# A hybrid decoder block on one core: another order of the first turnings, an earlier third product, later requests for the sums of h, and two sign products on ScalarE

## The chip, the cores and the metric

The kernel runs on one core of a Trainium2 chip. The metric is device time in microseconds (us), from start to end of one execution, for one problem size: 1024 tokens of 1024 channels, batch 1, all values float32.

## What is computed

The reference is one residual block with two token mixers side by side. Cut to what matters here:

```
mod = silu(c) @ w_ada + b_ada                       # shift, scale, gate
h = rmsnorm(x, norm_pre) * (1 + scale) + shift
u_pool, z_pool, u_ssm, z_ssm, g_pool, g_ssm = split(h @ w_in)        # 1024 x 6144
y_pool = causal_pool_mixer(u_pool, pool_w, pool_scale) * silu(z_pool)
y_ssm = s5_mixer(u_ssm, a_re, a_im, log_dt, b, c, d, glu) * silu(z_ssm)
merged = sigmoid(g_pool) * (y_pool @ w_branch_pool) + sigmoid(g_ssm) * (y_ssm @ w_branch_ssm)
out = x + gate * rmsnorm(merged @ w_out, norm_post)
```

The state-space mixer needs, for each of 64 groups and 64 states, powers and rotations of exp(dt * lambda). These tables ("coefficients") depend on small parameters only, and are made in the kernel.

## The kernel before

All large products are made with three matmuls each: both operands are split in a high part, rounded to the type that the matrix engine takes at full rate, and a low part, the rest; the products high x high, high x low and low x high are added in PSUM. ScalarE makes a high part by a copy (`split_hi`, `h_high`, `t_high`, `pair_high`), VectorE a low part by a subtraction (`split_lo`, `split_h`, `t_low`, `pair_low`). A product of one tile of 128 output channels takes eight steps (`k_step`, L1849), one for each tile of 128 input channels; a step is six matmuls of 512 columns.

The order of each engine's work is written out by hand, one list per engine, and semaphores join the lists. The lists that count here:

**First stage.** x comes in eight tiles of tokens. TensorE turns it to channels first by multiplying with diagonal matrices that hold the row scale (`transposed(k, tiles)`, L1874: tile k of the channels, eight matmuls). Turned tiles 0 and 1 lie in PSUM banks `ps0` and `ps1`, which products 0 and 1 use later; 2 to 7 go by turns through `psb` and `psa`, and ScalarE takes each out with `xt_out(k)` (L1003). Meanwhile VectorE sums the rows of `ada` (shift and scale) for tile k, ScalarE forms `h_of(k)` and `h_high(k)`, VectorE `split_h(k)`, and only then can step k of a product run. TensorE's list is: the turnings 0 to 3 for the first four token tiles, then for the last four, then for each k the step k of product 0 and of product 1 and the turning k + 4; the eight steps of product 2 stand behind steps 5 to 7 of the others (`third`). Product 2 uses `psa`, and its weights are split into `wx_hi`, `wx_lo`, which lie in the memory of `x_tok`, so that `split_hi(2)` waits for all turnings.

**Products 3 to 8** (`FIRST`: seven more of the gate, `gs`, and `zs 0`) follow each other. Weights of product n are split while product n-1 or n-2 runs; `split_hi(n)` stands in ScalarE's list behind the copy out of product n-2 (`evac`).

**Coefficients.** Between the splits, VectorE computes sine, cosine, magnitudes, factors and powers, 64 to 512 columns per operation (`reduced_angles` to `in_out_coefficients`, L530 to L644). When `cos_sin` has set `angle_ready`, GpSimd computes the rotations (`rotations`, L646, 78 operations) into another part of `coef`, and sets `tabled`. SyncE then stores `coef` (L732), after `coef_ready` and `tabled`. `coef` overlies `pair_raw0`, so that `load_pair(0)` waits for the end of that store.

**Sums of h.** The next eleven pairs of products are made by a Strassen-like scheme: seven half products P1 to P7 for each pair of output tiles, in the order P1, P2, P6, P5, P7, P4, P3. P5, P6, P7 and P4 need sums of quarters of h: `t_sums(k)` (VectorE, four operations), `t_high(k)` (ScalarE, 2048 columns) and `t_low(k)` (VectorE), for k = 0 to 3. The weights' side needs `sum1` to `sum4`, `pair_high` and `pair_low` per half product. P1 and P2 use h itself. TensorE's list has a wait for all four `t_low` ahead of the first P1. P2 of the first pair takes bank `ps1` and waits until ScalarE has copied out product 8 (`evac(("zs", 0))`, which stands in its list behind `pair_high` of P1, P2, P6 and P5).

Of the kernel before, what the change touches and what calls it, by code (L numbers as in the profile page):

```python
# [82 lines left out]
X_TILES_ACT, X_TILES_DVE = ((0, 1, 3), (4, 6, 7)), ((2,), (5,))  # L83

# [63 lines left out]
def build(nc, x, c_d, cols_d, consts_d, a_re_d, a_im_d, log_dt_d, bc_d, w_ada_d, wstream_d, pool_d, w_out_d, out):  # L148
    ctx = ExitStack()
    with ctx:  # L150
# [59 lines left out]
        wx_hi = at("wx_hi", [P, KT, P], b_at, F32R)  # L210
        wx_lo = at("wx_lo", [P, KT, P], b_at + TILE, F32R)
# [112 lines left out]
        xt = [ps[0], ps[1]] + [psb, psa] * 3  # L324
# [308 lines left out]
        def in_out_coefficients(steps):  # L633

            do, tt, ts, cmul, _ = s5_steps(nc.vector, steps)
            pr, pi, f_re, f_im = pw_re, pw_im, par["f_re"], par["f_im"]

            bf = lambda a: a.unsqueeze(2).broadcast_to((P, G, 8))
            cmul(coef[:, :, 0:8], coef[:, :, 8:16], pr[:, :, 1:9], pi[:, :, 1:9], bf(f_re), bf(f_im),
                 tmp_a[:, :, :], tmp_b[:, :, :])  # L640
            do(ts(coef[:, :, 8:16], coef[:, :, 8:16], sign, -1.0, ALU.mult, ALU.mult))

            do(ts(coef[:, :, 16:24], pr[:, :, 0:8], sign, None, ALU.mult))
            ts(coef[:, :, 24:32], pi[:, :, 0:8], -1.0, None, ALU.mult).then_inc(coef_ready, 1)  # L644
# [28 lines left out]
        def _(sp):  # L673
# [40 lines left out]
            for k in range(KT):  # L714
                if k in (1, 2):
                    load_w(k - 1)
                for f in range(2):
                    sp.dma_start(ada[:, 2 * (k // 4) + f, :, k % 4, :],
                                 w_ada_d.rearrange("(s k) p m -> k p s m", s=2)[k][:, :, f * HALF:f * HALF + HALF]).then_inc(ada_in[k], 16)
            load_w(2)  # L720
# [9 lines left out]
            sp.wait_ge(coef_ready, 1)  # L730
# [241 lines left out]
        def _(act):  # L972
            fn = nc.scalar.activation

            def split_hi(p):

                act.wait_ge(raw_in[p % 2], 16 * (p // 2) + 16)
                if p == 2:
                    act.wait_ge(xt_done, KT)
                elif previous(p) is not None:  # L980
                    act.wait_ge(mm_done, previous(p) + 1)
                fn((wx_hi if p == 2 else w_hi[p % 2])[:, :, :], raw[p % 2][:, :, :], ACT.Copy).then_inc(hi_done, 1)  # L982
# [20 lines left out]
            def xt_out(k):  # L1003

                act.wait_ge(xt_done, k + 1)
                fn(h_full[k][:, :], xt[k][:, :], ACT.Copy).then_inc(xt_taken, 1)

            def h_of(k):

                if k < 2:  # L1010
                    act.wait_ge(xt_done, k + 1)
                    src = xt[k]
                else:
                    act.wait_ge(xt_taken, k - 1)
                    src = h_full[k]
                act.wait_ge(mod_ready, 2 * k + 2)
                fn(h_full[k][:, :], src[:, :], ACT.Identity, bias=s_col[:, k:k + 1],
                   scale=g_col[:, k:k + 1]).then_inc(h_ready, 1)
# [6 lines left out]
            split_hi(0)  # L1025
            h_of(0)
            h_high(0)
            xt_out(2)
            split_hi(1)
            h_of(1)  # L1030
            xt_out(3)
            h_high(1)
            for k in range(2, KT):
                h_of(k)
                h_high(k)
                if k + 2 < KT:
                    xt_out(k + 2)
                if k == 5:
                    split_hi(2)
            act.wait_ge(h_done, KT)  # L1040
# [15 lines left out]
            for n in range(KT):  # L1056
# [7 lines left out]
                if n == 5:  # L1064
                    t_high(0)
                elif n == 6:
                    for k in range(1, 4):
                        t_high(k)
# [46 lines left out]

            pair_high(0, P1)
            pair_high(0, P2)
            pair_high(0, P6)
# [180 lines left out]
        def _(dve):  # L1299
# [59 lines left out]
            for k in range(KT):  # L1359
                scale_sum(k)  # L1360
                if k == 1:
                    split_h(0)
                shift_sum(k)
                if k > 1:
                    split_h(k - 1)
                if k < 2:
                    split_lo(k)
                if k == 6:
                    split_lo(2)
            split_h(KT - 1)  # L1370
            reduced_angles(steps)
            sine(steps)
            cosine(steps)
            split_lo(3)
# [34 lines left out]
            t_sums(0)  # L1409
            t_low(0)  # L1410
            t_sums(1)
            split_lo(8)
            t_sums(2)
            dve.wait_ge(tabled, 1)
            t_sums(3)
            for k in range(1, 4):
                t_low(k)
# [155 lines left out]

            sum1(0)
            sum2(0)
            pair_low(0, P1)
            pair_low(0, P2)
# [263 lines left out]
        def _(pe):  # L1841
# [32 lines left out]
            def transposed(k, tiles):  # L1874

                if k >= 4:
                    pe.wait_ge(xt_taken, k - 3)
                for t in tiles:
                    if k == 0:
# [6 lines left out]
            def step(n, k):  # L1886

                u = ("gs", n)
                if k == 0:
# [3 lines left out]
                    elif n == 2:  # L1893
                        pe.wait_ge(xt_taken, KT - 2)
# [5 lines left out]
            for tiles in (range(0, 4), range(4, CH)):  # L1900
                for k in range(4):
                    transposed(k, tiles)
            third = {5: (0, 1), 6: (2, 3), 7: (4, 5, 6, 7)}
            for k in range(KT):
# [4 lines left out]
                if k + 4 < KT:  # L1909
                    transposed(k + 4, range(CH))  # L1910
# [50 lines left out]
            pe.wait_ge(t_done, 4)  # L1961
            for j in range(NP):
                half_product(j, P1)
                half_product(j, P2)
                part_a(CHUNK_AT.get((j - 1, "b")))
# [184 lines left out]
```

## Time and profile before

| what | value |
|---|---|
| median of 3 runs | 972.71 us (972.57 to 974.25) |
| the profiled execution | 971.08 us, of which the span of the profile 969.3 us |
| TensorE busy | 941.6 us, 97% of the span |
| VectorE busy | 655.7 us, 68% |
| ScalarE busy | 348.6 us, 36% |
| GpSimd busy | 42.0 us, 4%, all of it between 68 and 113 us |
| granted clock of TensorE | 0.999 of full speed |
| chain that ended last | 89% on TensorE, 8% on VectorE |

The profile lists for each engine when an instruction started and how long it took, and, where the engine sat idle before it, how long and which instruction released it. Instructions of one engine overlap a little at their ends, so that the distance between two starts is often 0.1 us less than a duration. "The chain that ended last" goes back from the last instruction through whatever released each step. TensorE is busy in nearly all of the span, so the first question for any edit is which of its few idle stretches it touches.

### The profile page before, as it was taken

The page shows a single profiled execution, that of the slowest core. Times are in us where ns is not written, and L with a number is a line of the kernel's source. Part 1 is how long each engine was busy: PE and PEld are TensorE (multiplying, and loading weights), DVE is VectorE, ACT ScalarE, POOL GpSimd, SP SyncE. Part 2 cuts the span into 40 slices and gives each one's busy share as a digit, 9 for nine tenths or more (in the row PEclk, how much of TensorE's full clock was granted, in tenths as well). Part 3 has the DMA queues.
Part 4 walks back from the last instruction along what each step waited for, and adds up shares of the span by engine and source line. Part 5 has one row for each costly group of instructions (what it writes and reads, how often), then busy time and mean ns, then how long its engine had stood idle before and what let it go on. Part 6 is the DMA issues. An engine that isn't in the chain of part 4 may idle for free.

```text
span 969.3 us, 11612 instructions
## 1 busy us (share of the span) xinstructions
PE 941.6 (97%) x4448; PEld 789.1 (81%) x4448; DVE 655.7 (68%) x916; ACT 348.6 (36%) x404; POOL 42.0 (4%) x82
## 2 busy tenths in 40 slices
PE   3899989999999999999999999999999999999997
PEld 3788868888888888888888888888888888787886
DVE  5989898998888868766887667664344444355233
ACT  5841252223433344544454544631122231133111
POOL 0019600000000000000000000000000000000000
PEclk9999999999999999999999999999999999999999
DMA  9732463444455459657566544886542255322222
GB/s 346 293 135 84 161 223 140 155 153 153 155 188 190 164 198 260 200 169 216 173 198 200 164 139 135 278 327 226 174 166 109 95 220 192 130 88 87 87 87 87
DMA packets 95687, 168.27 MB, mean 174 GB/s; under 512 B 37648, under 2 KB 54160, under 8 KB 95632
## 3 DMA queue, kind: packets, MB, share of 16 engines
q1 hardware_dynamic: 86272, 163.07, 49.6%
q10 hardware_dynamic: 9360, 4.46, 2.1%
q8 instruction: 35, 0.57, 0.2%
q14 instruction: 20, 0.16, 0.1%
HBM read 118.21 MB, written 49.28 MB: 173 GB/s over the span
## 4 chain that ended last, share of the span: by engine, by line
PE 89%; DVE 8%; DMA 1%; ACT 1%; SPq 1%; issue 0%; DVEq 0%; ACTq 0%
PE ps L1855 49%; PE ps L1958 17%; PE ps L2058 8%; PE psb L1958 5%; PE ps L2004 2%; PE psb L1993 1%; PE psb L1991 1%; PE psa L1979 1%; PE psa L1927 1%; PE psa L1855 1%; DMA x_tok<-in_x 1%; DVE t_lo L1403 1%; DVE w_lo L1309 1%; DVE mod_out L1313 1%; PE psb L1927 0%; PE psa L1881 0%
## 5 line engine op out<-in xcount | busy, mean ns | idle before, releaser
L1855 PE MATMUL ps<-bop,w_hi 128*128 128x512 f32 x1312 | 352.6, 390 | 3.8 <-DVE bop L1357 2.2
L1855 PEld LDWEIGHTS ps<-bop,w_hi 128*128 128x128 f32 x1312 | 245.1, 188 | 55.6 <-issue 2.8
L1855 PE MATMUL ps<-bop,w_lo 128*128 128x512 f32 x656 | 202.0, 389 | 0.0
L1855 PEld LDWEIGHTS ps<-bop,w_lo 128*128 128x128 f32 x656 | 123.2, 188 | 25.6
L1309 DVE TENSOR_TENSOR w_lo<-raw,w_hi 128x1024 fp32r<-128x1024 f32 x49 | 60.1, 1227 | 57.6 <-ACT w_hi L982 57.4
L982 ACT ACTIVATE w_hi<-raw 128x1024 fp32r<-128x1024 f32 x49 | 51.7, 1057 | 94.3 <-PE ps L1855 84.4
L1958 PE MATMUL ps<-bop,r_hi 128*128 128x512 f32 x208 | 64.1, 389 | 0.0
L1958 PE MATMUL ps<-t_hi,r_hi 128*128 128x512 f32 x140 | 55.2, 394 | 0.0
L1958 PE MATMUL ps<-t_hi,r_lo 128*128 128x512 f32 x140 | 54.6, 390 | 0.0
L1958 PE MATMUL ps<-t_lo,r_hi 128*128 128x512 f32 x140 | 54.5, 389 | 0.0
L2058 PE MATMUL ps<-wo_hi,y_hi 128*128 128x512 f32 x128 | 49.9, 390 | 0.4 <-DVE wo_lo L1785 0.4
L2058 PE MATMUL ps<-wo_lo,y_hi 128*128 128x512 f32 x128 | 49.8, 389 | 0.0
L2058 PE MATMUL ps<-wo_hi,y_lo 128*128 128x512 f32 x128 | 49.8, 389 | 0.0
L1089 ACT ACTIVATE r_hi<-r_f 128x512 fp32r<-128x512 f32 x44 | 25.4, 622 | 67.0 <-DVE r_f L1510 65.5
L1958 PEld LDWEIGHTS ps<-bop,r_hi 128*128 128x128 f32 x208 | 39.0, 188 | 8.3 <-issue 0.3
L1773 DVE SCALAR_TENSOR_TENSOR y_raw<-gt,y_raw 128x1024 f32<-128x1024 f32 x8 | 9.8, 1226 | 47.9 <-ACT gt L1048 47.9
L1958 PE MATMUL ps<-bop,r_lo 128*128 128x512 f32 x104 | 40.5, 389 | 0.0
L1855 PE MATMUL ps<-y_lo,w_hi 128*128 128x512 f32 x128 | 39.4, 389 | 0.0
L1855 PE MATMUL ps<-y_hi,w_lo 128*128 128x512 f32 x128 | 39.4, 389 | 0.0
L1855 PE MATMUL ps<-y_hi,w_hi 128*128 128x512 f32 x128 | 39.4, 389 | 0.0
L1048 ACT ACTIVATE pu<-ps 128x1024 f32<-128x1024 f32 x9 | 17.6, 1955 | 57.9 <-PE ps L1855 57.9
L1821 DVE TENSOR_SCALAR stat<-stat 128x1 f32<-128x1 f32 x7 | 1.1, 154 | 49.0 <-ACT squares L1288 49.0
(311 smaller groups left out, 1542.2 us busy)
## 6 DMA issues: line engine op xcount, KB each, us to landing
raw<-in_wstream SPq DMA_DIRECT2D x58, 512.0 KB, 5.5
pair_raw<-in_wstream SPq DMA_DIRECT2D x22, 512.0 KB, 4.6
ada<-in_w_ada SPq DMA_DIRECT2D x16, 512.0 KB, 12.1
x_tok<-in_x SPq DMA_DIRECT2D x8, 512.0 KB, 6.3
gs_d<-gt SPq DMA_DIRECT2D x8, 512.0 KB, 4.9
win_d<-win_new SPq DMA_DIRECT2D x8, 512.0 KB, 3.9
wout_d<-wout_new SPq DMA_DIRECT2D x8, 512.0 KB, 5.6
wout<-wout_d SPq DMA_DIRECT2D x8, 512.0 KB, 4.1
```

The lines of the kernel that those rows point to most:

```text
L982: fn((wx_hi if p == 2 else w_hi[p % 2])[:, :, :], raw[p % 2][:, :, :], ACT.Copy).then_inc(hi_done, 1)
L1048: fn(dst, src, func, **kw).then_inc(job_out[slot(u)], 1)
L1089: fn(r_hi[o % RING // 4][:, o % 4, :].rearrange("p (k m) -> p k m", m=P), src, ACT.Copy).then_inc(pair_hi, 1)
L1309: tt(lo[:, :, :], raw[p % 2][:, :, :], hi[:, :, :].bitcast(F32), ALU.subtract).then_inc(raw_free[p % 2], 1)
L1313: return stt(scratch_, row, 1.0, halves(silu_row[:, :]), ALU.mult, ALU.mult, accum_out=acc)
L1403: tt(t_lo[:, k, :, :], t_f[:, k, :, :], t_hi[:, k, :, :].bitcast(F32), ALU.subtract).then_inc(t_done, 1)
L1773: stt(y_raw[:, n, :], gt[n % 2][:, :], 1.0, y_raw[:, n, :], ALU.add, ALU.mult).then_inc(gated, 1)
L1855: last = mm(ps[slot(u)][:, f * HALF:f * HALF + HALF], a[:, k, :], b(k, f), start=k == 0 and q == 0, stop=k == KT - 1 and q == 2)
L1927: last = mm(bank[:, at_:at_ + P + SG], vg, eye_c[:, g, :], start=True, stop=True)
L1958: last = mm(bank, a, b, start=k == 0 and q == 0, stop=k == 3 and q == 2)
L2004: last = mm(ps[slot(u)][:, f * HALF:f * HALF + HALF], a[:, 2 * q + k, :], b[:, k, f * HALF:f * HALF + HALF], start=k == 0 and p == 0, stop ...
L2058: ins = mm(ps[slot(("out", t))][:, f * HALF:f * HALF + HALF], a[:, k, t * P:t * P + P], b[:, f * HALF:f * HALF + HALF], start=first and q ...
```

## The change

It has five parts, all in the first 140 us.

1. TensorE's turnings go in the order 2, 0, 1, 3, 4, 5, 6, 7 (`XT_ORDER`). Turning 4 stands ahead of the first step of product 0, turning 5 ahead of the first step of product 1, 6 ahead of steps 1, and 7 ahead of steps 2. Tile 6 and 7 both use `psb`; turning 7 waits for five `xt_out`. ScalarE's list has `xt_out(2)` ahead of `h_of(0)`, and the others one place earlier.
2. The steps of product 2 stand behind steps 2 (two of them), 3, 5 and 7 of the others. `wx_hi` and `wx_lo` move to memory that is free by then, so that `split_hi(2)` no longer waits for the turnings; it stands behind `h_high(2)` and `split_lo(2)` behind `split_h(2)` (for k = 3 of the loop). SyncE asks for the third weight ahead of the `ada` tiles of k = 3, so that its wait for the freed buffer now stands ahead of ten of these loads.
3. On VectorE, `split_lo(3)` stands ahead of `cosine`. Two operations that multiply powers by a sign (512 columns each) leave VectorE; ScalarE does them as scaled copies behind `split_hi(7)`, and `coef_ready` counts to 2.
4. The order of the sums of h: VectorE has `t_sums(0)`, `split_lo(8)`, a wait for `coef_ready` at 2, `t_sums(1)`, `t_low(0)`, `t_sums(2)`, `t_low(1)`, the wait for `tabled`, `t_sums(3)`, `t_low(2)`, the low parts of P1 and P2, `t_low(3)`, and then `sum1`. ScalarE has `t_high(0)` and `t_high(1)` behind the copy out of product 6, `t_high(2)` ahead of the high parts of P1 and P2, and `t_high(3)` behind these two.
5. TensorE waits for the four `t_low` behind P2 instead of ahead of P1.

The diff, cut to its core:

```diff
@@ -81,6 +81,8 @@
 X_TILES_ACT, X_TILES_DVE = ((0, 1, 3), (4, 6, 7)), ((2,), (5,))
+XT_ORDER = (2, 0, 1, 3, 4, 5, 6, 7)
...
@@ -207,8 +209,8 @@
         x_tok = at("x_tok", big, b_at)
-        wx_hi = at("wx_hi", [P, KT, P], b_at, F32R)
-        wx_lo = at("wx_lo", [P, KT, P], b_at + TILE, F32R)
+        wx_hi = at("wx_hi", [P, KT, P], c_at + 5 * TILE, F32R)
+        wx_lo = at("wx_lo", [P, KT, P], rt_at + TILE, F32R)
...
@@ -321,7 +323,7 @@
-        xt = [ps[0], ps[1]] + [psb, psa] * 3
+        xt = [ps[0], ps[1], psb, psa, psb, psa, psb, psb]
...
@@ -638,10 +640,8 @@
                  tmp_a[:, :, :], tmp_b[:, :, :])
-            do(ts(coef[:, :, 8:16], coef[:, :, 8:16], sign, -1.0, ALU.mult, ALU.mult))
-            do(ts(coef[:, :, 16:24], pr[:, :, 0:8], sign, None, ALU.mult))
-            ts(coef[:, :, 24:32], pi[:, :, 0:8], -1.0, None, ALU.mult).then_inc(coef_ready, 1)
+            ts(coef[:, :, 8:16], coef[:, :, 8:16], sign, -1.0, ALU.mult, ALU.mult).then_inc(coef_ready, 1)
...
@@ -712,12 +712,11 @@
             for k in range(KT):
-                if k in (1, 2):
+                if k in (1, 2, 3):
...
                                  w_ada_d.rearrange("(s k) p m -> k p s m", s=2)[k][:, :, f * HALF:f * HALF + HALF]).then_inc(ada_in[k], 16)
-            load_w(2)
...
@@ -727,7 +726,7 @@
             store_gs(4)
-            sp.wait_ge(coef_ready, 1)
+            sp.wait_ge(coef_ready, 2)
...
@@ -975,9 +974,7 @@
                 act.wait_ge(raw_in[p % 2], 16 * (p // 2) + 16)
-                if p == 2:
-                    act.wait_ge(xt_done, KT)
-                elif previous(p) is not None:
+                if p != 2 and previous(p) is not None:
...
@@ -1002,13 +999,13 @@
-                act.wait_ge(xt_done, k + 1)
+                act.wait_ge(xt_done, XT_ORDER.index(k) + 1)
...
                 if k < 2:
-                    act.wait_ge(xt_done, k + 1)
+                    act.wait_ge(xt_done, XT_ORDER.index(k) + 1)
...
@@ -1023,20 +1020,22 @@
             split_hi(0)
+            xt_out(2)
...
             h_high(0)
-            xt_out(2)
+            xt_out(3)
...
             h_of(1)
-            xt_out(3)
+            xt_out(4)
             h_high(1)
+            xt_out(5)
...
                 h_high(k)
-                if k + 2 < KT:
-                    xt_out(k + 2)
-                if k == 5:
+                if k == 2:
                     split_hi(2)
+                if k in (2, 3):
+                    xt_out(k + 4)
...
@@ -1062,10 +1061,12 @@
                 if n == 5:
+                    act.wait_ge(coef_ready, 1)
+                    fn(coef[:, :, 16:24], pw_re[:, :, 0:8], ACT.Copy, scale=sign)
+                    fn(coef[:, :, 24:32], pw_im[:, :, 0:8], ACT.Copy, scale=-1.0).then_inc(coef_ready, 1)
+                if n == 6:
                     t_high(0)
-                elif n == 6:
-                    for k in range(1, 4):
-                        t_high(k)
+                    t_high(1)
...
@@ -1113,8 +1114,10 @@
+            t_high(2)
...
             pair_high(0, P2)
+            t_high(3)
...
@@ -1365,13 +1368,13 @@
                     split_lo(k)
-                if k == 6:
+                if k == 3:
...
             sine(steps)
+            split_lo(3)
             cosine(steps)
-            split_lo(3)
...
@@ -1407,14 +1410,15 @@
             t_sums(0)
+            split_lo(8)
+            dve.wait_ge(coef_ready, 2)
+            t_sums(1)
             t_low(0)
-            t_sums(1)
-            split_lo(8)
             t_sums(2)
+            t_low(1)
...
             t_sums(3)
-            for k in range(1, 4):
-                t_low(k)
+            t_low(2)
...
@@ -1571,10 +1575,11 @@
+            pair_low(0, P1)
+            pair_low(0, P2)
+            t_low(3)
...
             sum2(0)
-            pair_low(0, P1)
-            pair_low(0, P2)
...
@@ -1874,9 +1879,9 @@
                 if k >= 4:
-                    pe.wait_ge(xt_taken, k - 3)
+                    pe.wait_ge(xt_taken, 5 if k == 7 else k - 3)
                 for t in tiles:
-                    if k == 0:
+                    if k == XT_ORDER[0]:
...
@@ -1891,23 +1896,27 @@
                     elif n == 2:
-                        pe.wait_ge(xt_taken, KT - 2)
+                        pe.wait_ge(xt_taken, 4)
...
             for tiles in (range(0, 4), range(4, CH)):
-                for k in range(4):
+                for k in XT_ORDER[:4]:
                     transposed(k, tiles)
-            third = {5: (0, 1), 6: (2, 3), 7: (4, 5, 6, 7)}
-            for k in range(KT):
+            transposed(4, range(CH))
+            step(0, 0)
+            transposed(5, range(CH))
+            step(1, 0)
+            third = {2: (0, 1), 3: (2,), 5: (3,), 7: (4, 5, 6, 7)}
+            for k in range(1, KT):
+                if k + 5 < KT:
+                    transposed(k + 5, range(CH))
...
                     step(2, k3)
-                if k + 4 < KT:
-                    transposed(k + 4, range(CH))
...
@@ -1958,10 +1967,11 @@
-            pe.wait_ge(t_done, 4)
...
                 half_product(j, P2)
+                if j == 0:
+                    pe.wait_ge(t_done, 4)
...
```

## Rows read from the trace of the kernel before

**Rows 1.** which engine TensorE waited for: us in total, times, longest
```profile
PE psb L1958 <- DVE r_lo L1530: 2.5, 1, 2.5
PE ps L1855 <- DVE bop L1357: 2.2, 1, 2.2
PE ps L1855 <- DVE w_lo L1309: 1.5, 2, 1.1
```

**Rows 2.** timeline of TensorE, first stage: start us, us, instructions, idle before
```profile
26.18 1.15 PE L1855 MATMUL ps<-bop,w_hi 128*128 128x512 f32 x4 [2.15 <-DVE bop L1357]
...
30.36 1.95 PE L1881 MATMUL psb<-diag,x_tok 128*128 128x128 f32 x16
32.44 1.20 PE L1855 MATMUL ps<-bop,w_hi 128*128 128x512 f32 x4
...
67.89 1.07 PE L1855 MATMUL ps<-bop,w_hi 128*128 128x512 f32 x4
```

**Rows 3.** timeline of TensorE around its last long wait
```profile
136.59 0.70 PE L1958 MATMUL psb<-bop,r_hi 128*128 128x512 f32 x2 [2.51 <-DVE r_lo L1530]
...
139.51 0.70 PE L1958 MATMUL ps<-bop,r_hi 128*128 128x512 f32 x2
```

**Rows 4.** timeline of ScalarE from 60 us to 140 us
```profile
63.57 1.05 ACT L982 ACTIVATE w_hi<-raw 128x1024 fp32r<-128x1024 f32 x1
...
69.07 1.05 ACT L982 ACTIVATE w_hi<-raw 128x1024 fp32r<-128x1024 f32 x1
...
128.00 1.92 ACT L1054 ACTIVATE t_hi<-t_f 128x2048 fp32r<-128x2048 f32 x1 [0.61 <-DVE t_f L1398]
...
130.73 1.14 ACT L1089 ACTIVATE r_hi<-pair_raw 128x512 fp32r<-128x512 f32 x2
135.87 1.15 ACT L1089 ACTIVATE r_hi<-r_f 128x512 fp32r<-128x512 f32 x2 [4.01 <-DVE r_f L1510]
...
138.34 1.03 ACT L1048 ACTIVATE gt<-ps 128x1024 f32<-128x1024 f32 x1
```

**Rows 5.** timeline of VectorE from 70 us to 136 us
```profile
70.15 1.30 DVE L1309 TENSOR_TENSOR w_lo<-raw,w_hi 128x1024 fp32r<-128x1024 f32 x1 [1.94 <-ACT w_hi L982]
...
108.13 0.74 DVE L643 TENSOR_SCALAR coef<-pw_re,consts 128x512 f32<-128x512 f32 x1
...
127.82 6.69 DVE L1403 TENSOR_TENSOR t_lo<-t_f,t_hi 128x2048 fp32r<-128x2048 f32 x3
134.43 0.68 DVE L1504 TENSOR_TENSOR r_f<-pair_raw 128x512 f32<-128x512 f32 x1
```

**Rows 6.** timeline of GpSimd, whole program
```profile
68.28 0.24 POOL L651 COPY e_re<-par_w_cw 128x64 f32<-128x64 f32 x1 [67.84 <-DVE par_w_sw L584]
...
86.69 0.69 POOL L476 TENSOR_TENSOR tmp_d<-coef,e_im 128x256 f32<-128x256 f32 x1
...
90.36 1.09 POOL L475 TENSOR_TENSOR tmp_c<-coef,e_re 128x512 f32<-128x512 f32 x1
...
99.08 0.54 POOL L476 TENSOR_TENSOR tmp_d<-coef,e_im 128x64 f32<-128x64 f32 x1
...
103.16 0.88 POOL L477 TENSOR_TENSOR coef<-coef,e_im 128x128 f32<-128x128 f32 x1
...
109.34 0.82 POOL L478 TENSOR_TENSOR coef<-coef,e_re 128x256 f32<-128x256 f32 x1
110.23 1.59 POOL L479 TENSOR_TENSOR coef<-coef 128x256 f32<-128x256 f32 x1
111.91 1.06 POOL L480 TENSOR_TENSOR coef<-tmp_c,tmp_d 128x256 f32<-128x256 f32 x1
```

**Rows 7.** transfer issued at 18.01: size and us to landing
```profile
ada<-in_w_ada SPq DMA_DIRECT2D x1, 512.0 KB, 13.0
```

**Rows 8.** transfer issued at 113.11: size and us to landing
```profile
coef_d<-coef SPq DMA_DIRECT2D x1, 2560.0 KB, 8.1
```

**Rows 9.** transfer issued at 121.7: size and us to landing
```profile
pair_raw<-in_wstream SPq DMA_DIRECT2D x1, 512.0 KB, 5.9
```


## The prediction

> **What bounds the kernel now.** I read the waits of TensorE first. After its start it waits only a few times in the whole program [rows 1]: 2.2 us for the low part of the first tile of h, 1.5 us for low parts of weights (one of them 1.1 us, near 29 us), and 2.5 us for the low part of the first pair operand. Everything else is matmul behind matmul, so a change pays only where it removes such a gap, or costs where it opens one. Two stretches matter. First the stage that turns x and starts the first three products [rows 2]: TensorE idles 2.15 us before 26.18, runs without a gap from 32.44, and begins the fourth product at 67.89. Second the hand-over to the Strassen pairs [rows 3]: it idles 2.51 us before P1 at 136.59, and P2 starts at 139.51. Behind P2 the list of its waits has none as long as these, so the program's end moves as the start of P2 moves. That time is the one figure to work out.
>
> What releases P2 is not P1. P2 uses the bank of product `zs 0`, and ScalarE's queue holds the copy of that bank behind `pair_high` of P6 and P5, which wait for `sum1` and `sum2` on VectorE [rows 4]: P6 and P5 at 135.87, table load, copy at 138.34 for 1.03, P2 at 139.51. `sum1` began at 134.43, right behind three `t_low` of together 6.69 [rows 5]. So from `sum1` to P2 it is 5.08 us.
>
> **The first stage.** One turning is 16 records of the matmul, 1.95 with its tail and 1.8 without; between 32.44 and 67.89 lie three turnings and 22 steps of a product, so a step is (35.45 - 5.4) / 22 = 1.37 us [rows 2]. After the change turning 4 fills the gap of 2.15 before 26.18 (its bank is free, because tile 2 is turned and taken out first), and turning 5 fills the gap of 1.1 before the second product's first step. `xt_out(2)` now stands ahead of `h_of(0)` on ScalarE, and `h_of(0)` is ahead of the first step. It costs between 0 (the column that `h_of(0)` needs comes later anyway) and its own length, 1.03 for such a copy [rows 4]; taken 0.1, since that column comes from the first `ada` tile and is the last thing to arrive. The rest of the stage is the same steps and turnings in another order, so what the gaps took is what it gains: 2.15 + 1.1 + 0.4 in hand-overs. One new gap: turning 7 waits for `xt_out(6)`, behind `h_of(2)`, `h_high(2)` and the new `split_hi(2)` on ScalarE, some 0.5 us. Sum 3.65 - 0.1 - 0.5 = 3.1: the fourth product starts at 64.8 in place of 67.89, and each product behind it 3.1 earlier. Six products of 8 x 1.37 = 10.9 end near 130.5, where they now end at 136.59 - 2.51 = 134.1 [rows 3].
>
> SyncE: `load_w(2)` now waits for `raw_free` in front of ten loads of `ada`. The queue ahead of it is long (the second `ada` tile of k=3, issued at 18.01, lands 13.0 later, at 31.0 [rows 7]), so nothing runs dry; that tile lands one transfer later, 512 KB at the page's 346 GB/s, 1.5 us. Cost 0 to 1.5, taken 0: TensorE, with two steps of the third product put before it, comes to that tile of h only near 43. `store_gs` and the rest of SyncE's list are not passed by anything. Tile 7 of h is ready about 1 us earlier, since VectorE's wait for the high part of the third weight is gone.
>
> **VectorE and GpSimd.** Four things help VectorE. The split of the fifth weight was ready 1.94 us after VectorE wanted it [rows 5]; that wait goes, because it hung on the end of the third product (69.07 [rows 4]). The two sign products, 0.74 each with GpSimd beside them [rows 5], move to ScalarE, which is idle there. `t_low(3)` moves behind the low parts of P1 and P2. Alone these bring `sum1` 4 to 5 us forward. But `sum1` then has another predecessor: `t_low(3)` needs `t_high(3)`, which now stands behind `pair_high(0, P1)` and `(0, P2)` on ScalarE, and these need the first pair's weights. The weights overlie `coef`, so they are asked for only when `coef` is stored, and `coef` is stored when GpSimd has finished its rotations. In the kernel before, that chain had slack: GpSimd ends at 111.91 + 1.06 = 112.97 [rows 6], `coef` takes 8.1 [rows 8], the second half of the pair, issued at 121.7, lands 5.9 later at 127.6 [rows 9], while ScalarE read it only at 130.73 [rows 4]. From GpSimd's end to the pair's landing it is 14.6 us.
>
> With T the end of GpSimd, the chain after the change is: pair landed T + 14.6; P1's and P2's high parts 1.1 (1.14 for two [rows 4]); `t_high(3)` 1.92 [rows 4]; `t_low(3)` 2.2, a third of 6.69 [rows 5]; `sum1` to P2 5.08. With hand-overs of 0.05 that makes P2 = T + 24.95. Against 139.51, P2 breaks even at T = 114.55, that is if GpSimd ends 1.6 us later than now. If T only moves with its start (0.55 earlier, because the split of the fourth weight stands before `cosine` and comes 3.1 earlier), T = 112.4 and P2 = 137.4, a gain of 2.1.
>
> **Why GpSimd will end later.** Its operations take longer the wider VectorE's operation beside them is [rows 6]. One of 256 columns takes 0.69 beside one of 64, 0.82 beside a one-input operation of 512, 1.06 beside a two-input one of 512, and 1.59 beside a weight split of 1024; both lists run one for one in that stretch. I walked the two lists operation by operation with these prices. VectorE loses its waits and gets 2.2 to 2.8 us ahead of GpSimd's list, so each GpSimd operation meets a later and wider one:
> - up to its first operation of 512 columns (90.36 now): it also meets the split of the seventh weight (1.59 - 0.69 = 0.9) and six operations of 128 in place of 64 or of none: taken 1.9 in all;
> - six operations of 512 (1.09 now, beside 128) beside 256: 0.13 each, 0.8;
> - six of 64 (0.54 beside 256 now) beside 512: 0.54 + 0.27 = 0.81, six times, less the split of the seventh weight that met the first of them: 1.0;
> - six of 128 (0.88 now): the eighth weight's split is one of the partners (+0.5), and VectorE waits for the high part of the ninth weight for 1.5 us by my walk and leaves two of them free (-0.5): 0;
> - six of 256 (0.82 four times, 1.59, 1.06 now [rows 6]): one free, a split, four sums of h: 0.5;
> - its start: -0.55.
>
> The sum is +3.65: T = 116.6, and P2 = 141.6, 2.1 us later than now. Bounds: with none of the pairings changed T = 112.4; with every one of the last dozen operations beside one of 512 or 1024 columns, T = 118.5.
>
> The Trainium skill ("SBUF — State Buffer", "Who interferes with whom") states that a VectorE instruction with two SBUF inputs contends with a GpSimd instruction that reads SBUF, and that the second one fully blocks until the first is done; the trace agrees (1.59 for a GpSimd operation beside a 1024-column split). Read as that lock, the rule speaks against filling VectorE's waits in this stretch.
>
> The edits with one answer: the new places of `wx_hi`, `wx_lo` cost nothing by themselves. The two copies on ScalarE (0.57 each, as half of 1.14 for two of that size [rows 4]) lie between the split of the eighth weight and the next eviction, both far from late. `coef_ready` at 2 is a wait of VectorE ahead of `t_sums(1)`, with the whole of its list behind it, and of SyncE ahead of the store of `coef`; by my walk of the lists it is there 10 us before T. PE's `wait t_done` behind P2 costs nothing, since P2 is later than `t_low(3)`.
>
> **Rivals.**
> - A, the lock costs little (T between 112.4 and 114.5): P2 0 to 2 us earlier, 969.0 to 971.1 in a profiled run. For it: GpSimd starts earlier, and where VectorE waits GpSimd runs free. Against it: the prices of [rows 6].
> - B, the gains count in full because GpSimd ends before 112.5, or the pair's weights land sooner: P2 at 137.4 or less, 968.9 and below. For it only that the last sums of h and GpSimd's last operations may miss each other.
> - C, the other direction of the same place: GpSimd's last operation loses its turn to `t_low(0)`, 2048 columns wide (2.2), which now follows `t_sums(1)` directly. T = 119, P2 = 144, +4.5 us, 975.5. It decides from T above 116.8 on, which is near my sum.
> - D, SyncE's earlier wait starves the first stage: up to 1.5 us more before 65; it would come through T one for one, 974.7.
>
> **How the numbers follow.** The profiled execution took 971.08 (span 969.3 and 1.8 around it); the median of the runs shown is 972.71, 1.6 higher. Likeliest: 971.08 + 2.1 = 973.2 profiled, 974.8 as a median. Chances: forecast (T from 115.6 to 117.5, +1.1 to +3.1) 0.47; A and the part just above break-even 0.29; B 0.10; C 0.10; D 0.04. A measurement of this kernel can tell about 0.2% (1.9 us) from no change. The forecast straddles that line: somewhat more than half of it counts as slower, and with C and D that makes 0.45; faster 0.12; the same 0.43. As medians A lies at 970.7 to 972.7, C at 977.1, D at 976.3, B below 970.5. The range leaves out B and the best end of A, and takes in C: 971.0 to 977.3.
>
> **What would show it.** In the profile after: the fourth product's first matmul near 64.8; no wait of VectorE before the split of the fifth weight; GpSimd's last operation ending near 116.6, with its 64-column operations at 0.8 where they were 0.54; `t_high(3)` waiting for `pair_raw`, not for VectorE; TensorE idle about 3 us before P1 and about 6 us before P2, where it was 2.5 and 0.2. If GpSimd ends at 113 or before, the argument of the pairings is wrong and the kernel gains; if P2 starts without `t_high(3)` being late, the chain is wrong.

## The result, and the profile after

The changed kernel takes 975.27 us as a median of 11 runs, beside 972.13 for the kernel before: a ratio of 1.003, with a 95% interval of 1.0021 to 1.004 (one execution of the eleven, at 1614.81 us with a granted clock of 0.56 from end to end, is left out of the ratio). That is 3.1 us slower. The profiled execution took 974.41 us where that of the kernel before took 971.08.

| profiled execution | before | after |
|---|---|---|
| span of the profile | 969.3 us | 972.6 us |
| TensorE busy | 941.6 us | 943.0 us |
| GpSimd busy | 42.0 us | 45.3 us |
| fourth product begins | 67.89 | 65.10 |
| last operation of GpSimd ends | 112.97 | 116.07 |
| P2 of the first pair begins | 139.51 | 140.67 |
| P6 of the first pair begins | 142.35 | 145.45 |

The last row accounts for the result: from P6 on, both kernels run the same work, 3.10 us apart, and the spans differ by 3.3. So the question is how a first stage that gains 2.8 us ends in a hand-over that is 3.1 us late.

**TensorE's waits.** The page's list of what TensorE waited for in the kernel after (us in total, times, longest) answers [rows 1]:

```profile
PE ps L1967 <- ACT gt L1047: 5.8, 1, 5.8
PE psb L1967 <- DVE r_lo L1534: 1.3, 1, 1.3
PE ps L1860 <- DVE bop L1360: 0.7, 1, 0.7
```

The 2.2 us for the first tile of h became 0.7, the 1.5 for low parts of weights are gone, and the 2.5 before P1 became 1.3. One wait is new, and it is nearly as long as all of those together were (6.2): 5.8 us for ScalarE's copy of bank `zs 0`.

**The first stage** in TensorE's timeline after (start us, us, instructions, idle before), against [rows 2]:

```profile
26.47 1.16 PE L1860 MATMUL ps<-bop,w_hi 128*128 128x512 f32 x4 [0.68 <-DVE bop L1360]
...
36.00 2.05 PE L1886 MATMUL psb<-diag,x_tok 128*128 128x128 f32 x16 [0.22 <-ACT h_full L1003]
...
65.10 1.07 PE L1860 MATMUL ps<-bop,w_hi 128*128 128x512 f32 x4
```

Turning 4 fills the gap before the first step, turning 7 waits 0.22, and the fourth product starts 2.79 earlier.

**The hand-over** in TensorE's timeline after, against [rows 3]:

```profile
131.81 0.73 PE L1967 MATMUL psb<-bop,r_hi 128*128 128x512 f32 x2 [1.26 <-DVE r_lo L1534]
...
140.67 1.19 PE L1967 MATMUL ps<-bop,r_hi 128*128 128x512 f32 x2 [5.85 <-ACT gt L1047]
141.66 0.63 PE L1967 MATMUL ps<-bop,r_lo 128*128 128x512 f32 x1
142.08 1.05 PE L1967 MATMUL ps<-bop,r_hi 128*128 128x512 f32 x2
...
145.45 0.40 PE L1967 MATMUL ps<-t_hi,r_hi 128*128 128x512 f32 x1
```

P1 now starts 4.8 us earlier than before, but P2 1.16 later. And P2's matmuls are slow: two of them take 1.05 here and 0.62 in P1. P2 lasts 4.78 us (140.67 to 145.45), where it lasted 2.84 in the kernel before. The table by stretches says why. Its columns are the stretch, its length, TensorE's busy time, the granted clock as a share of full speed, and the DMA share and rate; first the kernel after, then the kernel before:

```profile
136.00:138.00 2.00, 0.00 (x0) 1.00 0.21 84
138.00:140.00 2.00, 0.00 (x0) 0.52 0.00 0
140.00:142.00 2.00, 1.33 (x3) 0.50 0.32 131
142.00:144.00 2.00, 2.00 (x6) 0.50 0.37 139
144.00:146.00 2.00, 2.00 (x8) 0.78 0.70 264
```

```profile
138.00:140.00 2.00, 2.00 (x9) 1.00 0.00 0
140.00:142.00 2.00, 2.00 (x10) 1.00 0.68 270
142.00:144.00 2.00, 2.00 (x11) 1.00 0.60 225
```

While TensorE sat idle, its clock was taken from 2.4 to 1.2 GHz (granted 0.50), and came back only after some 4 us of work. Together: 1.16 later, and 1.94 more for P2 at half the clock, are the 3.10 us.

**Where P2's start comes from.** The chain of work that ended last passes, in the kernel after, through GpSimd. On the page POOL holds 5% of it, where before it held none. Its pieces in order of time (start us, us, what):

```profile
115.01 1.07 POOL coef L482
116.21 8.07 DMA coef_d<-coef
124.30 0.33 SPq L697
124.68 5.70 DMA pair_raw<-in_wstream
130.42 0.51 issue
130.93 0.61 ACT r_hi L1090
131.55 1.81 ACT t_hi L1053
133.38 2.29 DVE t_lo L1406
135.68 0.61 DVE r_f L1508
...
138.21 1.28 ACT L1047
139.50 1.03 ACT gt L1047
140.53 0.14 issue
140.67 5.41 PE ps L1967 x14
```

This is the prediction's chain, link for link: GpSimd's end, store of `coef`, load of the pair, high parts, `t_high(3)`, `t_low(3)`, `sum1`, table load, copy, P2. From GpSimd's end to P2 it is 24.60 us.

**GpSimd's last operations** after, against [rows 6]:

```profile
91.62 1.15 POOL L477 TENSOR_TENSOR tmp_c<-coef,e_re 128x512 f32<-128x512 f32 x1
...
100.63 0.80 POOL L478 TENSOR_TENSOR tmp_d<-coef,e_im 128x64 f32<-128x64 f32 x1
...
106.55 0.89 POOL L479 TENSOR_TENSOR coef<-coef,e_im 128x128 f32<-128x128 f32 x1
...
110.51 0.64 POOL L478 TENSOR_TENSOR tmp_d<-coef,e_im 128x256 f32<-128x256 f32 x1
111.11 1.62 POOL L479 TENSOR_TENSOR coef<-coef,e_im 128x256 f32<-128x256 f32 x1
112.70 1.09 POOL L480 TENSOR_TENSOR coef<-coef,e_re 128x256 f32<-128x256 f32 x1
...
115.01 1.06 POOL L482 TENSOR_TENSOR coef<-tmp_c,tmp_d 128x256 f32<-128x256 f32 x1
```

The same operation of 64 columns takes 0.80 where it took 0.54. What VectorE has beside the last of these:

```profile
110.89 1.35 DVE L1312 TENSOR_TENSOR w_lo<-raw,w_hi 128x1024 fp32r<-128x1024 f32 x1 [2.05 <-ACT w_hi L979]
112.16 1.13 DVE L1396 TENSOR_TENSOR t_f<-h_full 128x512 f32<-128x512 f32 x1
```

In the last six of 256 columns one sees the price list at work: 0.64 while VectorE waits, 1.62 beside the split of a weight, 1.09 and 1.06 beside the sums of h.

### The profile page after: what moved, and what is told of

It reads as the page before. It is cut to its first block, busy times and chain, and to the rows that moved or that the text cites. A ratio compares the mean times of both kernels' runs of the same rounds, so it can differ in the third digit from the quotient of the medians.

```text
span 972.6 us, 11610 instructions
## 1 busy us (share of the span) xinstructions
PE 943.0 (97%) x4448; PEld 790.7 (81%) x4448; DVE 653.0 (67%) x914; ACT 349.7 (36%) x406; POOL 45.3 (5%) x82
## 3 DMA queue, kind: packets, MB, share of 16 engines
q10 hardware_dynamic: 9360, 4.46, 2.1%
## 4 chain that ended last, share of the span: by engine, by line
PE 87%; POOL 5%; DMA 3%; DVE 2%; ACT 2%; SPq 1%; issue 1%; DVEq 0%; ACTq 0%; POOLq 0%
PE ps L1860 48%; PE ps L1967 17%; PE ps L2068 8%; PE psb L1967 4%; PE ps L2014 2%; PE psb L2003 1%; PE psa L1989 1%; PE psb L2001 1%; DMA raw<-in_wstream 1%; PE psa L1936 1%; DMA coef_d<-coef 1%; POOL coef L482 1%; POOL coef L481 1%; POOL coef L479 1%; DMA pair_raw<-in_wstream 1%
## 5 line engine op out<-in xcount | busy, mean ns | idle before, releaser
L1534 DVE TENSOR_TENSOR r_lo<-pair_raw,r_hi 128x512 fp32r<-128x512 f32 x33 | 22.6, 687 | 17.5 <-ACT r_hi L1090 17.4
```

The source lines that it names most:

```text
L1534: tt(lo, full, hi.bitcast(F32), ALU.subtract).then_inc(pair_lo, 1)
```

## The experiments

The theory has three links: (1) VectorE's wider operations beside GpSimd's delay GpSimd's end; (2) that delay travels down the chain above to P2; (3) the idle stretch that this opens costs TensorE its clock. Only the first two were in the prediction. Each run below is named by its edit; times are medians of the device time, beside runs of the kernel before on the same chip, and the timeline figures are of the profiled execution. The kernel after was not run again beside them: a difference to it is taken from its median of 975.27, and comes out 0.2 to 0.3 us smaller if each median is first set against that of the kernel before beside it (972.13 for the kernel after, 971.94 and 971.80 here).

**Busy gap.** The kernel after, with matmuls whose result nobody reads put into the gap.

```diff
+                if j == 0:
+                    pe.wait_ge(job_out[2], 1)
+                    for n in range(24):
+                        mm(psa[:, 0:HALF], h[0](n % 4, 0)[:, 0:P], h[0](n % 4, 0), start=True, stop=True)
                 half_product(j, P2)
```

> The changed kernel, with 24 matmuls into a free bank (psa) between P1 and P2 of the first pair; their result is used by nobody. In the changed kernel TensorE idles 5.85 us there and the 12 matmuls of P2 then take 4.8 us (140.67 to 145.45) in place of 2.8. Theory 1 (the idle time costs TensorE its clock for a while): P2 still starts at 140.7, since ScalarE's copy of the bank releases it, but takes 2.8; the program is 2.0 us shorter than the changed kernel, 1.2 us longer than the one before. Theory 2 (P2's matmuls are slow for another reason, for example because of what ScalarE and VectorE do beside them): P2 takes 4.8 again and the time stays that of the changed kernel.

Measured: 972.66 us, a ratio to the kernel before of 1.0007 (0.9998 to 1.0016), 2.6 us less than the kernel after. TensorE does more work and the kernel is faster. In its timeline P2 starts as late as before, and is short again:

```profile
134.88 5.60 PE L1975 MATMUL psa<-bop 128*128 128x512 f32 x24
140.87 0.70 PE L1967 MATMUL ps<-bop,r_hi 128*128 128x512 f32 x2 [0.39 <-ACT gt L1047]
...
143.72 0.39 PE L1967 MATMUL ps<-t_hi,r_hi 128*128 128x512 f32 x1
```

P2 takes 2.85 us, and the granted clock is 1.00 in every stretch from 130 to 146. This shows link 3, and sizes it: P2 is 1.93 us shorter and P6 begins 1.73 earlier in the timeline, and the medians differ by 2.6.

**Tabled first.** The wait for GpSimd's end stands ahead of the split of the ninth weight, so that VectorE runs nothing beside GpSimd's last six operations.

```diff
             t_sums(0)
+            dve.wait_ge(tabled, 1)
             split_lo(8)
             dve.wait_ge(coef_ready, 2)
...
             t_low(1)
-            dve.wait_ge(tabled, 1)
             t_sums(3)
```

> The changed kernel with one wait moved: VectorE waits for GpSimd's end (tabled) ahead of the split of the ninth weight instead of ahead of t_sums(3). Lock theory: GpSimd's last four operations meet no wide VectorE operation (1.62, 1.09, 1.06, 1.06 now, 0.45 to 0.64 each then), so GpSimd ends at 113.9 in place of 116.07; VectorE's list has 3.7 us of waits behind it and catches up; the pair's weights, t_high(3) and P2 all move 2.1 us earlier, P2 at 138.5, and the idle time before it falls to 3.7 us. Time: 2.1 us less than the changed kernel, and up to 4.1 less if the clock then stays up. Rival (GpSimd's operations have their length by themselves): GpSimd ends at 116.1 again, VectorE's splits start later and nothing is gained, 0 to 1 us lost.

Measured: 973.21 us, ratio 1.0013 (1.0004 to 1.0022), 2.1 less than the kernel after. GpSimd's timeline ends so:

```profile
111.05 0.65 POOL L478 TENSOR_TENSOR tmp_d<-coef,e_im 128x256 f32<-128x256 f32 x1
111.65 0.65 POOL L479 TENSOR_TENSOR coef<-coef,e_im 128x256 f32<-128x256 f32 x1
...
113.78 0.73 POOL L482 TENSOR_TENSOR coef<-tmp_c,tmp_d 128x256 f32<-128x256 f32 x1
```

An added wait of 5.75 us on VectorE makes the kernel faster: the operations take 0.65 in place of 1.62, GpSimd ends at 114.51, 1.56 earlier (2.1 was expected), and P2 starts at 139.16, 1.51 earlier. The delay goes down the chain one for one. P2 still pays for the clock (4.46 us after an idle of 5.45), so links 2 and 3 are separate.

**Sums first.** `t_low(3)` goes behind `sum1` and `sum2`, where it doesn't hold the copy.

```diff
             pair_low(0, P2)
-            t_low(3)
             sum1(0)
             sum2(0)
+            t_low(3)
```

> The changed kernel with t_low(3) behind sum1 and sum2 on VectorE. If P2 is released by the chain pair_raw - high parts of P1 and P2 - t_high(3) - t_low(3) - sum1 - sum2 - high parts of P6 and P5 - copy of bank ps1, then taking t_low(3) and its wait (1.03 + 2.2) out of it moves P2 3.3 us earlier, to 137.4; TensorE idles 2.6 us before it. Time: 3.3 us less than the changed kernel, up to 5.3 less if the clock stays up, which is 0.2 to 2 us under the kernel before. Rival (P2 waits for something else as well, as t_low or the loads): less than 1 us.

Measured: 970.73 us, ratio 0.9986 (0.9978 to 0.9995), 4.5 less than the kernel after. P2 starts at 137.51 after an idle of 2.51, and lasts 4.17 us, with a granted clock of 0.70 and 0.50 in the stretches from 138 and 140. P2's start moved by 3.16: one link of the chain, `t_low(3)` of 2.3 us with the wait of 1.03 before it, was there only by the order of a list.

**Copy first.** ScalarE's copy of bank `zs 0` goes ahead of the high parts of P6 and P5.

```diff
             t_high(3)
-            pair_high(0, P6)
-            pair_high(0, P5)
             act.wait_ge(gs_stored[0], 16 * 4)
             evac(("zs", 0), gt[0][:, :], ACT.Silu)
+            pair_high(0, P6)
+            pair_high(0, P5)
```

> The changed kernel with ScalarE's copy of product 8's bank (zs 0) ahead of the high parts of P6 and P5. The bank is complete at 130, so the copy no longer hangs on sum1 and sum2: P2 follows P1 at 134.6 without a gap, and the wait moves to P6, which needs sum2 (137.0), its high part, sum4 and its low part: P6 near 138.5, 1 us idle. In the kernel before, P6 starts at 142.35. Time: 3.9 us less than the kernel before, 7 us less than the changed one (which loses 2 us of it to the slow P2). Rival (t_low(3), which ends at 135.6, and the copy ahead of the high parts delay P6 beyond 140): 2 us or less under the kernel before.

Measured: 967.85 us, ratio 0.9954 (0.9941 to 0.9966): 7.4 us less than the kernel after and 4.1 less than the kernel before. Its timeline of TensorE:

```profile
131.94 0.74 PE L1967 MATMUL psb<-bop,r_hi 128*128 128x512 f32 x2 [1.60 <-DVE r_lo L1534]
...
135.97 0.69 PE L1967 MATMUL ps<-bop,r_hi 128*128 128x512 f32 x2 [0.97 <-ACT gt L1047]
...
138.82 0.40 PE L1967 MATMUL ps<-t_hi,r_hi 128*128 128x512 f32 x1
```

P2 4.70 earlier and 1.93 shorter make 6.63, and the profiled executions differ by 6.62 (974.41 and 967.79). With that move the change is a gain.

**Copy first, alone.** The same move on the kernel before.

> The kernel before, with one move: ScalarE's copy of bank zs 0 stands ahead of the high parts of P6 and P5, as in e4. Theory: in the kernel before P1 and not the copy held this place (TensorE idle 2.51 us before P1 for the low part of P1's weights, 0.2 us before P2), so the move that was worth 7.4 us on the kernel after is worth almost nothing here: P2 at 139.3 in place of 139.51, 0 to -0.3 us. Rival: the copy's place is a cost of its own in both kernels, and the move brings 1 us or more here too.

Measured: 971.71 us, ratio 0.9996 (0.9987 to 1.0006): no difference that can be told. The copy's place is free where P1 itself comes late, and worth 7.4 us where P1 comes early. It is a debt that the change calls in. The run's profile shows something else. TensorE idles before P1 as long as in the kernel before, 2.50 us here and 2.51 in [rows 3], but here the clock falls, P1's matmuls are slow, and P2 starts at 140.46 where 139.3 was expected:

```profile
136.00:138.00 2.00, 1.74 (x4) 0.50 0.51 209
138.00:140.00 2.00, 2.00 (x7) 0.70 0.13 53
```

**First stage only.** The kernel before with parts 1 and 2 of the change.

> The kernel before with parts 1 and 2 of the change alone (order of the turnings, third product earlier, its weights split and loaded earlier); the coefficients' order, the sums of h and the sign products as before. TensorE starts the fourth product 2.8 us earlier, as in the changed kernel. GpSimd's list is untouched. Lock theory: VectorE gets ahead of it all the same, so GpSimd ends near 115.8 instead of 112.97, and the pair's weights land near 130.4. sum1 waits for them (131.5) and P2 starts near 136.6, 2.9 us earlier than in the kernel before; the program is 2.9 us shorter. Rival (GpSimd keeps its length): it ends at 112.4, the pair is there at 127, sum1 follows t_low(3) at 131.4, and the time is the same: so GpSimd's end is what tells them apart, not the total.

Measured: 969.13 us, ratio 0.997 (0.9959 to 0.998), a gain of 2.7 us. P1 starts at 133.39, 3.20 earlier than in [rows 3]. Here GpSimd ends at 113.83, 0.86 later than before, and not at the 115.8 that the walk gave. With the old order of the sums VectorE waits 2.04 us for `t_high(0)` up to 113.16, and GpSimd's last three operations run free (0.64, 0.73, 0.73). The gain arrives although the pair's weights come later, because they had slack. In this profile, too, the clock falls after an idle of 2.00 us: P1 takes 4.41 us, and of the 3.20 only 1.80 are left where P6 begins (140.55).

**Sums' order only.** The kernel before with parts 4 and 5.

> The kernel before with parts 4 and 5 alone (order of the sums of h on VectorE and ScalarE, the wait for t_low behind P2); the first stage and the sign products as before. VectorE's list up to the eighth split is that of the kernel before, so GpSimd ends at 113.0 as there and the pair lands at 127.6. P1 starts right behind the ninth product, at 133.7, 2.9 us earlier than before; P2 is bound by pair - high parts - t_high(3) - t_low(3) - sum1 - copy and starts near 138.3, with 1.9 us of idle time. 1.2 us less than the kernel before. Rival (the new order alone is what costs): P2 at 140 or later, slower than before.

Measured: 974.61 us, ratio 1.0016 (1.0005 to 1.0028), where 1.2 us less than the kernel before was expected: a miss. Its profiled execution, 972.37 us, has GpSimd's end at 113.06 and P2 at 138.68, which is 0.83 earlier than before, and after an idle of 2.50 us P2 lasts 4.41 us, most of it at half the clock, so that P6 begins 0.74 later than in the kernel before. The chain gave the start of P2 within 0.4 us, and in this execution the clock took more than the gain. The twelve executions fall in two groups, five from 970.6 to 972.4 us with a mean granted clock of 0.997 to 0.999, and seven from 974.6 to 975.1 with 0.994 to 0.996. The profiled execution, with the fall in it, belongs to the first group. So that fall alone is not what sets the second group apart; no profile of the second group was taken, and what costs it another 2.4 us or so stays open.

**Sign products only.** The kernel before with the two products on ScalarE.

> The kernel before, with nothing of the change but the two sign products on ScalarE. Theory: VectorE's list is 2 x 0.74 = 1.5 us shorter, nothing else changes in front of sum1 (the pair's weights have 3.1 us of slack), so sum1 starts near 133.0, P1 near 135.1 and P2 near 138.0: -1.5 us. Rival, the lock alone: VectorE comes earlier to its last wide operations, GpSimd ends about 1 us later, and the move gives nothing because its time was spent in a wait of VectorE for t_high(0) (2.04 us at 116.88): then P2 stays within 0.3 of 139.5.

Measured: 970.9 us, ratio 0.9991 (0.9982 to 1.0001). The medians differ by 1.5 us (972.44 beside it), the ratio says 0.9, and its interval goes from a gain of 1.7 to none. The timeline lies between the two theories. `sum1` begins at 133.80, 0.63 earlier, out of the 1.5 us taken from VectorE's list. The rest went to the lock. Two more of VectorE's sums of h now run beside GpSimd, at 1.22 and 1.11 us where the kernel before had 0.68 and 0.69 for them, and GpSimd ends at 113.66, 0.7 later. After an idle of 2.39 us the clock falls here too: P1 begins 0.63 earlier than in [rows 3], at 135.96, but takes 4.40 us, and P2 follows at 140.36, so that this profile hides the gain that the medians suggest.

**No rotations.** The kernel after, with GpSimd's 78 operations replaced by one fill; the rotations aren't computed.

```diff
-            rotations(steps)
+            steps.do(nc.gpsimd.memset(coef[:, :, 32:80], 0.5))
             pool.sem_inc(tabled, 1)
```

> The changed kernel with GpSimd's 78 operations replaced by one memset; the rotations are left out, so the tables of the state-space mixer are wrong. Lock theory: VectorE's operations from 68 us on have their lengths without GpSimd (0.3 for 128 columns, 0.6 for 512), coef is stored from 105.5 on (when ScalarE has made the sign products), the pair lands near 119.5, t_high(3) and the sums no longer wait for it, P1 starts right behind the ninth product at 130.3 and P2 near 134. The program is 5.4 us shorter than the one before and 8.5 shorter than the changed kernel. Rival (the chain through coef is not what binds, VectorE is): P2 at 137 or later, 2.5 us or less under the kernel before.

Measured: 967.0 us, ratio 0.9951 (0.9937 to 0.9966), 8.3 less than the kernel after. VectorE's sums of h all take 0.68 or 0.69 now. Its timeline, first here, then in the kernel after at the same operation:

```profile
113.47 0.68 DVE L1399 TENSOR_TENSOR t_f<-h_full,t_f 128x512 f32<-128x512 f32 x1
```

```profile
114.26 1.22 DVE L1399 TENSOR_TENSOR t_f<-h_full,t_f 128x512 f32<-128x512 f32 x1
```

The pair's high parts start at 122.73 without a wait, and P2 at 134.96, after an idle of 1.45 us. P2 is 5.71 earlier and, at the full clock, 1.94 shorter. So GpSimd's presence costs the kernel after some 8 us: by its place at the head of the chain, by its hold on VectorE, and by the clock that the idle stretch loses.

**All mended.** The kernel after with the three moves above, and on ScalarE `t_high(2)` ahead of the copy out of product 7 and `t_high(3)` ahead of the high parts of P1 and P2.

> The changed kernel with all that the runs point to: the wait for GpSimd's end ahead of the ninth weight's split, t_low(3) behind sum1 and sum2, t_high(2) ahead of the copy out of product 7 (which waits for a store), t_high(3) ahead of P1's and P2's high parts, and the copy out of product 8 ahead of the high parts of P6 and P5. GpSimd ends at 114.5, the pair lands at 128.9, P1 starts at 130.8, P2 at 133.7 and P6 at 136.6 where the kernel before has 142.35; no idle time over 1 us, so the clock stays up. 5.7 us less than the kernel before (966.3). If the waits only move to P6 or P5 (t_low(3), sum4), 4 us less, as with the copy alone.

Measured: 965.62 us, ratio 0.9937 (0.9925 to 0.9948), 6.2 us less than the kernel before and 9.7 less than the kernel after. P6 starts at 137.00, the granted clock is 1.00 in every stretch from 130 to 146, and behind the start this is the whole list of TensorE's waits:

```profile
PE ps L2069 <- DVE wo_lo L1791: 0.4, 1, 0.4
PE psb L1887 <- ACT h_full L1003: 0.3, 1, 0.3
PE ps L1861 <- DVE bop L1361: 0.2, 1, 0.2
```

## Why the prediction was right, and where it wasn't

The forecast was a small loss, 974.8 us; the median is 975.27. Step by step:

| step | predicted | measured |
|---|---|---|
| fourth product begins | 64.8 | 65.10 |
| GpSimd's last operation ends | 116.6 | 116.07 |
| from there to P2 | 24.95 | 24.60 |
| P2 begins | 141.6 (+2.1) | 140.67 (+1.16) |
| P2's duration | as before, 2.84 | 4.78 |
| profiled execution | 973.2 | 974.41 |
| median against profiled execution | +1.6 | +0.9 |

**The first stage.** The gaps went as said. Of the 3.1 us, 2.8 came. The first step keeps an idle of 0.68 that the sum took as filled, while turning 7 waited 0.22 and not 0.5. Alone the stage is worth 2.7 us in the medians (*first stage only*), so rival D, SyncE's wait starving it, is out.

**VectorE and GpSimd.** The mechanism is shown from three sides: by the prices in the rows, by *tabled first*, where a wait of VectorE frees GpSimd, and by *no rotations*, where VectorE's slow operations vanish with GpSimd's. The Trainium skill ("SBUF — State Buffer", "Who interferes with whom") says that a VectorE instruction with two SBUF inputs and a GpSimd instruction that reads SBUF block each other, and this case agrees in both directions: a GpSimd operation of 256 columns takes 0.64 while VectorE waits and 1.62 beside a split; a VectorE sum of 512 columns takes 0.68 alone and up to 1.22. The walk, term by term, from the starts of the operations in both timelines:

| stretch of GpSimd's list | predicted | measured |
|---|---|---|
| its start | -0.55 | -0.21 |
| up to its first operation of 512 columns | +1.9 | +1.47 |
| six of 512 | +0.8 | +0.56 |
| six of 64, with the two fills before them | +1.0 | +0.78 |
| six of 128 | 0 | +0.46 |
| six of 256 | +0.5 | +0.04 |
| sum | +3.65 | +3.10 |

The signs are right, and most pairings were priced a little too high. The last two terms missed in opposite ways: VectorE's wait for the ninth weight left three operations free, as the walk had it, but one of 128 columns and two of 256, where it had two and one. One figure of the range is off by arithmetic: T = 117.5 makes P2 2.9 us later, not 3.1. Rival A (the lock costs little) and rival B are out. Rival C needed T above 116.8 and stayed away: `t_low(0)` began at 116.54, behind GpSimd's end.

**The chain.** Every link stands in the chain above, and `t_high(3)` waited for nothing but its predecessors on ScalarE, whose high parts waited 1.92 us for `pair_raw`, as said. The two products on ScalarE took 0.74 and 0.62 at 104.12 and delayed nothing. Two sights were wrong without consequence. TensorE's idle before P1 was to be about 3 us and is 1.26, since P1 starts as soon as its own high and low part are made, 1.4 us behind the landing of the weights, and waits for none of P2's. And nothing was said of `t_high(2)`, which stood behind a copy that waited 7.01 us for a store of `gs`; `t_low(2)` waited 2.42 for it.

**The step that failed** is in the first paragraph: "the program's end moves as the start of P2 moves". That takes P2's duration as given. The prediction itself put an idle of about 6 us ahead of P2 and went on with full-speed matmuls behind it. The idle measured 5.85, and P2 took 1.94 us more; that term was in no sum and no rival. *Busy gap* shows it alone. Of the 3.1 us, 1.16 came by the way that was predicted. That the forecast still came within 0.5 us is luck: other errors stood against it: 0.9 less on P2's start and 0.7 less on the median's distance from the profiled execution, beside 1.9 more for the clock.

**The distance between median and profile** may have its reason in the same term. The kernel before idles 2.5 us ahead of P1. In its profiled execution the clock stays at 1.00 through that; in the profile of *copy first, alone*, with the same idle, it falls, and in that of *sign products only*, with 2.39, too. Over the 65 executions of the kernel before that were taken beside the experiments, the 20 with a mean granted clock of 0.999 or more average 971.2 us, and the 23 with 0.997 or less 972.7. So part of the kernel before's executions probably pay a fall that its profile doesn't show. The profiled execution of the kernel before was then one of the lucky ones, and its rows hold no sign of the term that was missed. That this is what separates the executions is inferred from clock and time together, and wasn't shown by a profile of a slower one.

**Whose the loss is.** Parts 1 and 2 are a gain of 2.7 us, part 3's sign products a gain of about 0.9 that can't be told from none, and parts 4 and 5 alone a loss of 1.6 by the ratio. The effects don't add: GpSimd's end moved by 0.9 with the first stage, 0.1 with the sums' order, 0.7 with the sign products, and by 3.1 with all of them, where together they leave VectorE fewer waits in which GpSimd runs free. That this is why they don't add was not tested by itself. Nor was the other half of part 3, the split of the fourth weight ahead of `cosine`: it is in the kernel after and in none of the single runs, and may hold a share of what is missing.

## What to carry to other kernels

Filling one engine's waits can be a loss when those waits were what let another engine run; look which operations stand side by side before and after, and give the one that heads a chain of transfers the free time. When an edit makes an early wait of TensorE vanish, follow the next one by name. Here it was a copy behind two unrelated operations in a list, worth nothing before and 7 us afterwards. And price an idle stretch of TensorE twice, once for its length and once for the slow matmuls behind it.

## What the runs showed of the hardware

- After an idle of 5.85 us the granted clock was 0.50, and P2 took 4.78 us in place of 2.84; after 5.45 us (*tabled first*), 4.46. In the first of these it came back to 1.00 some 4 us after work had begun again. The Trainium skill ("TensorE: Matmul & The Clock Gate", "Part 1: The HAM clock gate (the "warmup" mystery)") says the same: the throttled level is the default, and activity releases it.
- After a short idle the fall varies from profile to profile: none after 2.51 us in the profile of the kernel before, a fall after 2.50 (*copy first, alone*), 2.50 (*sums' order only*), 2.51 (*sums first*), 2.39 (*sign products only*) and 2.00 us (*first stage only*), none after 1.60 and 0.97 (*copy first*). A fall may come while TensorE is already working again: in *sums first* the first matmuls of P2 ran at full speed, 0.69 and 0.40 us, and later ones at half.
- 24 matmuls that nobody needs, 5.60 us of them in the gap, made the kernel 2.6 us faster.
- A wait of VectorE added beside GpSimd (5.75 us, *tabled first*) made it 2.1 us faster.
